# RWKV-7 recurrence: 128x128 blocks in four units and a sample unit, or 64x64 quadrant blocks in three units

## What is computed

```
def rwkv_step(S, inp):
    r_t, w_t, k_t, v_t, kk_t, b_t = inp
    sa = jnp.einsum('bhvk,bhk->bhv', S, -kk_t)
    S = S * w_t[:, :, None, :] + sa[..., None] * b_t[:, :, None, :] + v_t[..., None] * k_t[:, :, None, :]
    return S, jnp.einsum('bhvk,bhk->bhv', S, r_t)
```

```
    yn = ((y - mean) * lax.rsqrt(var + GN_EPS)).reshape(B, T, R_WIDTH) * gn_g.astype(f32) + gn_b.astype(f32)
    bonus = (jnp.sum(r_f * k_f * rk.astype(f32), axis=-1, keepdims=True) * v_f).reshape(B, T, R_WIDTH)
    out = (yn + bonus) * g
```

## Time and profile before

| | us |
|---|---|
| median of 3 runs (lowest, highest) | 5376.59 (5369.36, 5382.99) |
| profiled execution: span from first to last instruction | 5363.1 |
| PE busy in it | 4322.0 (81%) |
| DVE, ACT, POOL busy | 2140.0, 1460.6, 470.6 |
| one pair, first transpose of its recurrence to the first of the next pair's | 241.2 |
| of that the recurrence and norm, up to the next dense product | 174.0 |

### The profile page before, as it was taken

How to read it: one execution, slowest core, us unless ns; L and a number is a source line. 1 busy time by engine, 2 the same in 40 slices (tenths; PEclk the granted TensorE clock), 3 DMA queues, 4 the chain that set the end, 5 groups by cost and what they waited for, 6 DMA issues and landing times. The chain is left out here.

```text
span 5363.1 us, 77650 instructions
## 1 busy us (share of the span) xinstructions
PE 4322.0 (81%) x25724; PEld 3905.9 (73%) x25724; DVE 2140.0 (40%) x3451; ACT 1460.6 (27%) x2837; POOL 470.6 (9%) x470
## 2 busy tenths in 40 slices
PE   4876878787686699999758768787876767999995
PEld 3855767666576599999657657666765756999995
DVE  3253444434333343333443434434443424333334
ACT  3243131322134421111232421322222334111113
POOL 0010212121200000000000112112121000000000
PEclk7967878788798899999878778888887988999997
DMA  4100000000020011111121000000002000111111
GB/s 156 38 11 21 1 19 1 19 2 21 33 73 32 16 40 47 47 43 47 35 92 30 14 15 2 18 10 10 18 5 82 30 25 24 44 46 47 43 47 48
DMA packets 211117, 181.56 MB, mean 34 GB/s; under 512 B 17524, under 2 KB 194884, under 8 KB 210080
## 3 DMA queue, kind: packets, MB, share of 16 engines
q1 hardware_dynamic: 199392, 128.60, 8.1%
q0 software_dynamic: 11456, 49.58, 2.4%
HBM read 152.50 MB, written 25.65 MB: 33 GB/s over the span
## 5 line engine op out<-in xcount | busy, mean ns | idle before, releaser
L565 PE MATMUL PS<-HH,WH 128*128 128x352 f32 (+1 forms) x3680 | 1206.4, 328 | 83.5 <-PEq L549 83.5
L565 PE MATMUL PS<-HH,WL 128*128 128x352 f32 (+1 forms) x3680 | 1190.6, 324 | 0.0
L565 PE MATMUL PS<-HL,WH 128*128 128x352 f32 (+1 forms) x3680 | 1188.6, 323 | 0.0
L565 PEld LDWEIGHTS PS<-HH,WH 128*128 128x128 f32 x3680 | 704.4, 191 | 103.8 <-issue 101.0
L1099 ACT COPY R<-PS 128x256 f32<-128x256 f32 (+9 forms) x843 | 324.8, 390 | 1640.4 <-ACTq L1112 578.5
L565 PEld LDWEIGHTS PS<-HH,WL 128*128 128x128 f32 x3680 | 705.7, 192 | 1.3 <-issue 0.8
L565 PEld LDWEIGHTS PS<-HL,WH 128*128 128x128 f32 x3680 | 703.6, 191 | 0.0
L1664 DVE TENSOR_TENSOR WL<-WRAW,WH 128x1024 fp32r<-128x1024 f32 x226 | 293.2, 1297 | 868.6 <-DVEq L1663 868.6
L1099 ACT CAST WH<-WRAW 128x1024 fp32r<-128x1024 f32 x234 | 245.5, 1049 | 611.9 <-ACTq L1104 611.9
L556 PE MATMUL PS<-CST,R 128*128 128x128 f32 (+3 forms) x944 | 162.2, 330 | 236.4 <-PEq L549 236.3
L1067 PE MATMUL PS<-GL,WH 128*128 128x352 f32 x1056 | 339.6, 322 | 0.0
(11 more groups left out here) (254 smaller groups left out, 6126.2 us busy)
## 6 DMA issues: line engine op xcount, KB each, us to landing
WRAW<-in_w_gate_up SPq DMA_DIRECT2D x88, 512.0 KB, 3.7
WRAW<-in_w_down SPq DMA_DIRECT2D x46, 512.0 KB, 3.5
WRAW<-in_w_in SPq DMA_DIRECT2D x38, 512.0 KB, 3.7
x_spill<-R POOLq DMA_DIRECT2D x2, 4224.0 KB, 12.6
R<-mix_dram POOLq DMA_DIRECT2D x16, 528.0 KB, 7.3
R<-x_spill POOLq DMA_DIRECT2D x2, 4224.0 KB, 19.8
WRAW<-in_w_mem_kv SPq DMA_DIRECT2D x16, 512.0 KB, 3.5
WRAW<-in_w_out SPq DMA_DIRECT2D x16, 512.0 KB, 3.5
```

The lines of the kernel that those rows point to most:

```text
L565: ins = e.matmul(out, lhs(k, wp), rhs(k, xp), start=first, stop=(k == n - 1 and xp == 1))
```

## The change

The 128x128 blocks with two zero quadrants are replaced by their 64x64 diagonal quadrants, kept compact: a buffer of 128 partitions by 384 columns holds 12 blocks, chunk parity a in the partition half, and tile x and head h along the columns. There are three units of 384 tokens (`XU` = 3 tiles of 128). The 32 sample tokens become chunk 4 of the last unit, padded with zeros, with a state of its own (`SBDS[1]`), so the sample unit is gone. `STEPS` lists the chunk steps of each unit: 6, 6 and 5. `per_block` issues 12 products of 64x64x64, with the two halves a next to each other.

```diff
-UNITS = SEQ // 256
+UNITS = 3
+XU = 3
+UW = 2 * XU * 64
...
+    STEPS = ((0, 1, 2, 3, 4, 5), (0, 1, 2, 3, 4, 5), (4, 0, 1, 2, 3))
+    B_TOK, B_NEW, B_LOW, B_T1, B_DX, B_DXT, B_PTS, B_Q, B_MV = 0, 2, 0, 2, 0, 1, 2, 4, 4
+    B_YT, B_U, B_DS, B_Y = 3, 5, 6, 7
...
+            def quadrants():
+                return [(x, h, a) for x in range(XU) for h, a in ((0, 0), (1, 1), (0, 1), (1, 0))]
...
+            def per_block(b, left, right, start=True):
+
+                for x in range(XU):
+                    for h in range(2):
+                        for a in range(2):
+                            at = b * 512 + (2 * x + h) * HEAD
+                            ins = e.matmul(PS[half(a), at:at + HEAD], left(a, x, h), right(a, x, h), start=start(x, h) if callable(start) else start,
+                                           stop=True, skip_group_check=True)
+                return ins
...
+            def level_left(u, n):
+                POOL_PE.wait(e, ("elf", u, n))
+                DVE_PE.wait(e, ("x", u, n))
+                PE_ACT.tell(per_block(B_T1, lambda a, x, h: grp(ELF[n], a, x, h), lambda a, x, h: grp(XX, a, x, h)), ("t1", u, n))
...
+                for n in range(LEVELS):
+                    if n == LEVELS - 1 and s > 0:
+                        outputs(s - 1)
+                    level_left(s, n)
+                    if n < 4:
+                        d_of(n + 2)
+                    level_right(s, n)
+                    if n < 3:
+                        u_of(n + 3)
+                solved(s)
```

```diff
+            def norm_root(u):
+                DVE_ACT.wait(e, ("var", u))
+                e.activation(YSTD, YVAR, ACT.Ln, bias=CST[:, C_EPS + 1:C_EPS + 2], scale=1.0 / HEAD).then_inc(S("act_done"), 1)
                 e.wait_ge(S("act_done"), 1)
                 e.sem_inc(S("act_done"), -1)
+                ACT_DVE.tell(e.activation(YSTD, YSTD, ACT.Exp, scale=-0.5), ("rstd", u))
```

More of the change, by code:

```diff
@@ new lines, in level_right @@
+            def level_right(u, n):
+                ACT_PE.wait(e, ("t1", u, n))
+                if n == 0:
+                    POOL_PE.wait(e, ("xt", u))
+                else:
+                    DVE_PE.wait(e, ("xt", u, n))
+                if n < LEVELS - 1:
+                    PE_DVE.tell(per_block(B_DX, lambda a, x, h: grp(XT, a, x, h), lambda a, x, h: grp(T1, a, x, h)), ("dx", u, n))
+                PE_DVE.tell(per_block(B_DXT, lambda a, x, h: grp(T1, a, x, h), lambda a, x, h: grp(XT, a, x, h)), ("dxt", u, n))
@@ new lines, in solved @@
+            def solved(u):
+                DVE_PE.wait(e, ("xt", u, LEVELS))
+                for x in range(XU):
+                    for h in range(2):
+                        for a in range(2):
+                            at = (B_PTS + a) * 512 + x * HEAD
+                            ins = e.matmul(PS[half(h), at:at + HEAD], ATM[half(a), x, half(h)], grp(XT, a, x, h), start=True, stop=True)
+                PE_ACT.tell(ins, ("pts", u))
+                ACT_PE.wait(e, ("mv", u))
+                PE_ACT.tell(per_block(B_Q, lambda a, x, h: grp(XT, a, x, h), lambda a, x, h: MVS[half(a), x, half(h)]), ("q", u))
@@ L1358, in by_token @@
-                give(e, "tm_ready")
-                e.wait_ge(S("mv_psum"), 1)
-                e.sem_inc(S("mv_psum"), -1)
-                copy(MVS[0:n, 0:tiles, :], PS[0:n, 1536:1536 + tiles * P].rearrange("p (x t) -> p x t", x=tiles)).then_inc(S("act_done"), 1)
+                for x in range(XU):
+                    PE_ACT.wait(e, ("tm", u, x))
+                    copy(ATM[:, x, :], bank(x, 0, P))
+                    ACT_PE.tell(copy(bkv(u)[:, x, :, :], bank(x, P, 512).rearrange("p (a t) -> p a t", a=3)), ("tm", u, x))
@@ new lines, in chunk_state, with by_head @@
+            def chunk_state(s, c):
+                _, _, _, at, state = chunk_at(s - 1, c)
+                e.wait_ge(S("decayed"), 1)
+                e.sem_inc(S("decayed"), -1)
+                PE_DVE.wait(e, ("ds", s, c))
+                DVE_PE.tell(e.scalar_tensor_tensor(out=state, in0=bank(B_DS, 0, P), scalar=EC[:, 20 + at:21 + at], in1=STMP,
+                                                   op0=ALU.mult, op1=ALU.add), ("s", s, c))
+            groups = [P, 2 * XU, HEAD]
+            def by_head(buf):
+                return buf.rearrange("p (g t) -> p g t", t=HEAD)
@@ L1969, in low, with norm_centre @@
+            def norm_centre(u):
+                PE_DVE.wait(e, ("y", u))
+                y = by_head(bank(B_Y, 0, UW))
+                e.tensor_reduce(YSUM, y, AX.X, ALU.add).then_inc(S("dve_done"), 1)
                 e.wait_ge(S("dve_done"), 1)
                 e.sem_inc(S("dve_done"), -1)
[L1971 to L1981 removed]
```

705 lines of the change are left out of this document (342 added, 363 removed).

## The result

The changed kernel takes 4929.9 us (median of 4 runs, 4916.4 to 4944.1) against 5374.2 for the kernel before beside it (4 runs, 5369.4 to 5383.0): a ratio of 0.9172, with a 95% interval from 0.9151 to 0.9192. A repeat gave 0.9151 (0.9137 to 0.9164), 4919.0 us; the experiments are measured against this repeat. Ratios and their intervals are taken from fast executions alone and medians from all, which matters only in run 3, where four of ten executions are slow.

The account below looks back on a forecast made before the run. PE was taken as the bound; slots of 34.8, 44.8 and 48.3, tail 25 and start 0.6 gave 153.5 us a pair against 174.0, 164 us less in eight pairs: 5212 us from 5376.6, range 4950 to 5400.

Parts of the forecast that it names:

- The bound, and where the change acts: Whole kernel: PE limits; only the recurrence and norm, 174.0 us a pair in eight pairs, can move.
- The price of a 64x64 product: PE, two products at a time: a group of twelve takes about 0.9 us at 2.4 GHz, 1.55 at 1.2.
- rival A: Recurrence levels: clock stays at 2.4 GHz, 121.1 us a pair, 4954 us in all; chance 0.20.
- slot 1: Second unit's stretch of a pair's recurrence: head 11.3, levels 30.8, solved 2.7, together 44.8 us.
- slot 0: First unit's stretch of a pair's recurrence: head 7.6, levels 24.5, solved 2.7, together 34.8 us.
- slot 2: Third unit's stretch of a pair's recurrence: 48.3 us, with 3.5 added for ACT's table loads.
- tail: End of a pair's recurrence: five uncovered chunk steps, 14 us, then the exposed last norm; 25 us in all.
- dense stretch, and start: Dense work behind each recurrence, left alone at 67.2 us, and an extra evacuation at the start, 0.6 us.
- A level at 2.4 GHz: One level of a unit's solve, products, copy, subtraction and hand-overs between PE, ACT and DVE: 3.5 us.
- Slot 2's stall: Third unit: PE's transposes of the normed output wait for ACT's two table loads ahead of the levels, 3.5 us.
- Rival C: per_block: the two halves of a pair, writing one bank, take turns; 226 us a pair, 5793 us; chance 0.13.
- Rival B: Whole recurrence: clock stays at 1.2 GHz throughout, 167.0 us a pair, 5321 us; chance 0.22.

Follow-up runs that it names:

- run 3: run 2 plus three unread 128x128 products in levels 1 to 4 while PE waits for ACT's copy: 5340.6 us, 0.9880.
- run 2: Changed kernel with per_block's loop order turned over, all six products of the array's upper half, then all six of the lower: 5380.5 us, 1.0005.
- run 5: Changed kernel with a second semaphore instruction behind each of the 253 counted waits of a pair: 5076.4 us, 0.9431.
- run 10: Changed kernel with one square root on ACT and a reciprocal on DVE in place of the head norm's logarithm and exponential: 4864.0 us, 0.9043.
- run 9: Changed kernel with PE's loop over the four pairs written out, so no branch back between pairs: 4874.0 us, 0.9054.
- run 12: Changed kernel with 20 unread products ahead of the recurrence, 5 behind the sample state's transpose, four bank claims moved ahead: 4883.0 us, 0.9074.
- run 6: run 5 with a semaphore for each waiting engine in the added instruction, in place of one shared by all four: 5065.0 us, 0.9428.

## Why the prediction was wrong

**The bound, and where the change acts: right.** PE's work in the recurrence was the place. The pair read closely gave 50.1 us in period (241.2 to 742.09 - 551.03 = 191.1), and eight times that is 401 of 421. The last pair of each layer gave more: from its first transpose to the next product of the dense helper it took 233.7 us before and takes 166.3 now, which is 12 us more than in the pair read closely (174.0 to 118.7). Why isn't shown.

**The price of a 64x64 product: right.** Two at a time, 0.9 us for a group at 2.4 GHz and 1.55 at 1.2, came out as 0.92 and 1.54.

**The failed step: "the likeliest case has the heads at 2.4 GHz and the levels at 1.2, since the blocks are between the 128x128 that held 2.4 GHz and the 32x32 that did not, and PE now stands idle in each level."** It cost 32 us a pair, the distance from 153.5 to rival A's 121.1. The measured sum is 118.7. Runs 2 and 3 show what I had ordered wrongly. I sorted by the size of a block and by PE's idle time. Two 64x64 blocks side by side, four in the scores, held 2.4 GHz through slot 1 with 16% of idle time, and the same blocks one after another fell to 1.2 there with 8%. What fits these runs is that it counts how much of the array works at a time. It is an inference, with two marks against it: one at a time held 2.4 GHz through the levels of slot 0 (run 2), and added full products did not keep slot 0 from falling in two pairs of run 3. The 0.57 of the sample unit, on which I leaned, were blocks of 32x32 (a sixteenth of the array each). That the halves overlap I had read and used for the price, but not for the clock.
The Trainium skill (TensorE: Matmul & The Clock Gate, Part 1) says that the clock follows how busy PE has been recently. Going by the busy time of the records, run 2 beside the changed kernel disagrees with that: 80% (6.92 of 8.65 us) ahead of the fall, against 75% (6.01 of 8.05) where the clock held.

**Margins of the clock.** The forecast's instinct that idle time threatens the clock was not empty: with 0.08 to 0.25 us more at each hand-over (run 5) slot 1 fell to 0.68. The changed kernel lies on the good side of an edge, not far from it.

| term, us | forecast | rival A | measured |
|---|---|---|---|
| slot 0 | 34.8 | 26.6 | 27.7 (24.6 in the repeat) |
| slot 1 | 44.8 | 32.7 | 29.8 |
| slot 2 | 48.3 | 36.2 | 36.5 |
| tail | 25 | 25 | 24.7 |
| dense stretch, and start | 67.2 + 0.6 | 67.2 + 0.6 | 72.3 (68.7) |

**A level at 2.4 GHz, 3.5 us: measured 3.15.** The hand-overs were the error. "0.15 to 0.2 us each way" came from the earlier trace rows, where each has its second instruction; counted, PE to ACT takes 0.04 and ACT to PE 0.05. With a `chunk_u` it is 4.03 against 4.2.

**"Counted waits drop an instruction each, most of them beside waiting; I take nothing for them": wrong.** Doubling them costs 157 us. By symmetry that is the order of what they gave: about 12 us a pair directly, and the rest by keeping the clock. It isn't a measurement of the kernel with hand-overs written back in full, which wasn't tried.

**Slot 2's stall, 3.5 us: found as 4.75**, in the place named. That it comes from the two table loads was largely wrong: without the second load and its function it is still 3.80 (run 10).

**The tail, 25 us: right by luck, since two errors cancel.** Five chunk steps were put at 14 us and take 10.5 (645.86, the first L937, to 656.40), since they run at 2.4 GHz for most of the way. Missing was PE's branch back to the head of the loop, 4.2 us bare (run 9). "Before, the next dense product waited for none of the root" was seen, but not that the branch also ran under those last products, as the kernel before shows:

```profile
714.06 3.86 PE L975 MATMUL PS<-TMP,CST 128*128 128x352 f32 x6 [2.27 <-PEq L549]
718.24 0.63 PE L565 MATMUL PS<-HH,WH 128*128 128x352 f32 x1 [0.32 <-PEq L549]
```


**The dense stretch: "67.2 of dense work that the change leaves alone"** was wrong by 1.5 to 5.1 us a pair. The same code took 72.3 us at a clock of 0.81 and 68.7 at 0.87. In run 12, with PE kept busy at its end, it takes 66.8 at 0.97, of which 1.0 us is the earlier claims. So most of this is the clock too.

**Rival C is refuted.** The Trainium skill (TensorEngine Tiling (Array Packing), Restrictions and Gotchas) says that different row tiles can't access the same PSUM bank at the same time. The pairs of `per_block` do: one bank, different partitions, 0.92 us for 24 records together and 1.43 apart (run 2). Rival B is refuted by the clock of 1.00.

The range missed by 20 us at its lower end, which was set at rival A's sum. Rival A's span, 5363.1 - 423 = 4940, is within 3 us of the profiled 4942.5, partly by luck: the recurrence is 2.4 us a pair shorter than A had it, the dense stretch 5.1 longer, and the last pair of each layer gave more. What lies between 4954 and 4929.9 is the step from span to median. The forecast added the 13.5 us of the kernel before; here the profiled execution was the slowest of four, and the median is 12.6 below its span. The executions of the changed kernel spread from 4898.8 to 4944.1 us over both measurements, and the range left no room for that below A.

## What to carry to other kernels

Order small products so that neighbours lie in different parts of the array, in rows and in columns: it gives the overlap, and here it kept the clock up as well, which in slot 1 was worth more than the overlap (17 of the 26 us between 55.5 and 29.8, by the 38.7 of run 3). When a kernel's levels are short chains between engines, count the semaphore instructions on the path: each is a tenth to a quarter of a microsecond, and the clock may fall with them. And where PE must wait for some microseconds ahead of a stretch that decides, products that nobody reads are worth trying; an edit that shortens the path may give nothing until the clock is held.

## What the runs showed of the hardware that was not expected

- The clock was 0.59 in a slot with PE busy for 92% of it, one quadrant at a time, and 1.00 at 84% with two (run 2). With three products of full width in each of four levels it was 0.96 (run 3). In slot 0 the same order had 1.00 through its levels in run 2, and 0.58 in one pair of run 3 with the added products.
- A second semaphore instruction behind a wait costs 0.08 us on ACT, 0.10 on DVE and 0.25 on PE (run 5), whether or not engines share the semaphore (run 6).
- Going back to the head of PE's pair loop leaves PE idle for 4.1 to 4.5 us when nothing covers it, and 0.4 to 0.5 us is left without the loop (run 9).
- Logarithm and exponential each load a table, 1.28 us apiece, in every unit's norm (616.89 and 618.59).
- The same binary's slot 0 takes 24.5 or 27.7 us, pair by pair, by when the clock rises; it is 23.0 each time when PE is busy before.
